# A sorted, alternating list of experts, and TensorE work moved into the waits of the expert stage

## The chip, the cores and the metric

The kernel runs on one core of a Trainium2 chip. The metric is the device time of one execution in microseconds, the median of three runs.

## What is computed

A decoder layer for one sequence of 512 tokens and a width of 1024, all in float32. A first part (modulation from a vector c, a gated recurrence with a causal convolution beside causal pooling, an output projection, the residual sum) leads to `h`, the normed and modulated rows that go into a mixture of experts:

```
logits = h @ router_w + router_b              # 512 x 32
top_val, top_idx = top_k(logits, 4)           # four experts a token
gates = softmax(top_val)
for each expert e, on the rows that chose it:
    u = h_rows @ w1[e] + b1[e]                # 1024 -> 2048
    a = min(u_even, 7) * sigmoid(1.702 * min(u_even, 7)) * (clip(u_odd, -7, 7) + 1)
    y = a @ w2[e] + b2[e]                     # 1024 -> 1024
f = sum over a token's four experts of gate * y
out = x + gate_f * rms_norm(f)
```

512 tokens with 4 choices make 2048 rows, spread unevenly over 32 experts. The number of rows of each expert is known only when the router has run.

## The kernel before, in words

**Ahead of the expert stage.** The first part runs on all engines to about 245 us. Then the routing: VectorE takes the four largest logits of each token, TensorE counts by products with ones and an upper triangle how many rows each expert has and where each row stands in its expert, and VectorE turns this into slots (L1074 to L1095). Rows of one expert are packed into halves of H = 32 rows; two halves are a step of 64. TensorE makes the table of slots (L1393, 16 products that follow the pairs of VectorE operations of L1094 and L1095), VectorE the indices for gathers and scatters (L1124 to L1129, semaphore `idx_ok`). A small table in SBUF, `counts`, has for each expert the steps (row 0), the halves (row 1), the full steps of two halves (row 2), and in row 3 how much the semaphore of its weights rises (16, or 0 for an expert without rows). All engines read it into registers and loop over it.

**The expert stage.** Every engine runs the experts in the order 0 to 31, two to a turn of its loop (`pair` and `slot`), and skips those without rows. For an expert TensorE does, in this order:

- the bias product (L1497): a selection matrix `sel_e`, made by VectorE for this expert (`select`, L1160), times `b1_all`, into bank 7; ScalarE copies it to `b1_cur` (L821);
- for each full step the up products of both halves (`up`, L1418, 32 matmuls a half; each float32 matmul has two records in the profile), and between them the transposes of the next step's gathered rows (`transpose_x`, L1406) and the turn of the first activated half (`turn_first`, L1427);
- for an odd last half its up products, the same transposes, a wait for its activation (`act_ok`) and the turn;
- a register load of the next expert's halves (`load_halves`, L1477);
- for each full step the turn of the second half (`turn(1)`), the down products of the first half (`down`, L1446, 16 matmuls a half, four weight tiles of four), the down products of the second, with the turn for the next step inside; for an odd last half its down products.

VectorE adds the bias, clamps, multiplies and stores the activated half to `act_store` (`activate`, L1139 to L1147), and adds the two parts of each down result (`finish`, L1152 to L1156). ScalarE does the sigmoid, copies turned blocks (`take_gT`, L798) and transposed rows (`take_xT`, L789). GpSimd gathers rows two steps ahead (L575, L580), copies the next two halves into the first two places of `act_store` (L634, semaphore `copied`), and scatters results (L586, L590).

**The weights.** `W1` has two slots of eight tiles of 1 MB; expert e goes into slot e mod 2. SyncE issues them (`load_w1`, L372): tile k waits until the last up half of expert e - 2 has passed tile k (`w1_used`, L359). `W2` has one slot of four tiles of 1 MB; ScalarE issues them (`load_w2`, L377), tile by tile behind the last down half of the expert before (`w2_used`). Expert 0's weights are loaded before the stage. Expert 1 would go to slot 1, which is free: four tiles behind `counts_ok`, four behind `idx_ok`. It has no rows in these inputs, so nothing is loaded for it there.

```
436            sp.wait_ge(counts_ok, 4)
440            load = sp.value_load(counts[0:1, 3, 1:2], min_val=0, max_val=16)
441            with sp.If(load > 0):
443                    load_w1(sp, 1, 1, k)
```

Of the kernel before, what the change touches and what calls it, by code (L numbers as in the profile page):

```python
# [5 lines left out]
def hybrid_layer(nc, x, c, w_ada, b_ada, norm_mix_pre, norm_mix_post, w_in, conv_w, conv_b, gate_a_w, gate_a_b,  # L6
# [10 lines left out]
    P = 128  # L17
    T, D = x.shape[1], x.shape[2]
# [20 lines left out]
    VECS = 72  # L39

# [13 lines left out]
    with ctx:  # L54
# [126 lines left out]
        idx_n = take(NQ).bitcast(i32)  # L181

# [15 lines left out]
        counts = OV[0:1, 6656 - 4 * E:6656].rearrange("p (a e) -> p a e", a=4).bitcast(i32)  # L198
# [92 lines left out]
        b1_in = sem("b1_in")  # L291
        bias_const = sem("bias_const")
# [88 lines left out]
        def _(sp):  # L381
# [43 lines left out]
            load = sp.value_load(counts[0:1, 3, 1:2], min_val=0, max_val=16)  # L425
            with sp.If(load > 0):
                for k in range(HALF):
                    load_w1(sp, 1, 1, k)
            sp.wait_ge(idx_ok, 1)
            with sp.If(load > 0):  # L430
                for k in range(HALF, KT):
                    load_w1(sp, 1, 1, k)
# [6 lines left out]
            sp.reg_add(landed[1], landed[1], load)  # L439
# [14 lines left out]
            with sp.Fori(1, E // 2) as pair:  # L454
                for slot in range(2):
                    e = 2 * pair + slot
                    add_steps(bass.ds(e - 2, 1))
                    load = sp.value_load(counts[0:1, 3, bass.ds(e, 1)], min_val=0, max_val=16)
                    with sp.If(load > 0):
# [5 lines left out]
                        for k in range(KT):  # L465
# [7 lines left out]
                            load_w1(sp, e, slot, k)  # L473
# [18 lines left out]
        def _(pool):  # L492
# [55 lines left out]
            nc.gpsimd.iota(iota_t, [[0, J], [1, H]], base=0, channel_multiplier=0, **IMP).then_inc(route_const, 1)  # L548
            nc.gpsimd.iota(iota_e, [[1, E]], base=0, channel_multiplier=0, **IMP).then_inc(route_const, 1)
# [108 lines left out]
        def _(act):  # L658
# [157 lines left out]
            def expert(e):  # L816
                n_halves = act.value_load(counts[0:1, 1, e], min_val=0, max_val=T // H)
                n_full = act.value_load(counts[0:1, 2, e], min_val=0, max_val=T // (2 * H))
                with act.If(n_halves > 0):
                    act.wait_ge(b1_ps, act.snap(biased, min_val=0, max_val=E) + 1)  # L820
                    nc.scalar.activation(b1_cur, b1_bank[:, :], ACT.Copy).then_inc(b1_ok, 1)  # L821
                    act.reg_add(biased, biased, 1)
# [37 lines left out]
            with act.Fori(0, E - 1) as e:  # L860
                expert(bass.ds(e, 1))
                load = act.value_load(counts[0:1, 3, bass.ds(e + 1, 1)], min_val=0, max_val=16)
                with act.If(load > 0):
# [3 lines left out]
                    for part in range(J):  # L867
# [10 lines left out]
                        load_w2(act, e, part, w2_v[1:E])  # L878
# [18 lines left out]
        def _(dve):  # L897
# [133 lines left out]
            def route_tile(i):  # L1031

                dve.wait_ge(evac, number["logits", i] + 1)
                if i == 0:
                    dve.wait_ge(router_in, 32)
                    dve.wait_ge(route_const, 5)
# [554 lines left out]
```

## Time and profile before

| what | value |
|---|---|
| median of three runs | 1470.37 us (1470.14 to 1477.83) |
| the profiled execution: its own time | 1479.31 us |
| its span, first to last instruction | 1477.6 us |
| TensorE busy | 1231.0 us (83%) |
| VectorE, ScalarE, GpSimd busy | 412.6, 217.1, 276.5 us |
| moved by the DMA queues | 462.84 MB, mean 313 GB/s |
| granted TensorE clock, mean | 0.907 of 2.4 GHz |

Rows of the profile name a source line of the kernel before, the engine, what is written and read, and how often. PE is TensorE, DVE VectorE, ACT ScalarE, POOL GpSimd, SP SyncE. "Idle before" is the time the engine stood still in front of an instruction, with the engine, the tile and the line that ended it. PEclk is the granted clock, 1.00 for 2.4 GHz and 0.50 for 1.2.

### The profile page before, as it was taken

How to read it: one execution, taken by the hardware profiler on the slowest of the kernel's cores; microseconds unless marked ns; L12 is line 12 of the kernel's file. 1: busy time of each engine (PE TensorE's matmuls, PEld its weight loads, DVE VectorE, ACT ScalarE, POOL GpSimd, SP SyncE). 2: the span in 40 equal slices, each digit the busy share in tenths (PEclk: the TensorE clock that was granted, in tenths of full speed). 3: DMA queues.
4: the chain of work that ended last, by engine and by line, in shares of the span. 5: the costliest groups of instructions: out<-in, count | busy, mean ns of one | idle time of the engine just before them, and what ended most of it. 6: DMA issues, size and time to landing. Idle time of an engine off the chain costs nothing.

```text
span 1477.6 us, 28341 instructions
## 1 busy us (share of the span) xinstructions
PE 1231.0 (83%) x8843; PEld 416.9 (28%) x8844; DVE 412.6 (28%) x864; ACT 217.1 (15%) x481; POOL 276.5 (19%) x421
## 2 busy tenths in 40 slices
PE   4999995468998999877757999986799889989961
PEld 1434455112332333221212333321223223322320
DVE  3215336212232232211112222321132222222317
ACT  2108532001110111100001101110011011101101
POOL 3032001201222122211101211321021112211212
PEclk9899995688999999988868999998799999999975
DMA  9882514597659588899999970599998997899354
GB/s 323 308 298 115 235 43 185 222 420 297 243 209 420 226 357 341 361 419 421 419 421 420 419 306 25 236 387 420 400 404 363 421 421 325 328 421 421 139 212 183
DMA packets 77461, 462.84 MB, mean 313 GB/s; under 512 B 11924, under 2 KB 12052, under 8 KB 29312
## 3 DMA queue, kind: packets, MB, share of 16 engines
q1 hardware_dynamic: 49280, 314.72, 52.5%
q10 hardware_dynamic: 17568, 126.14, 20.7%
q0 software_dynamic: 10592, 21.72, 4.3%
q8 instruction: 11, 0.18, 0.1%
q14 instruction: 10, 0.08, 0.0%
HBM read 453.08 MB, written 16.91 MB: 318 GB/s over the span
## 4 chain that ended last, share of the span: by engine, by line
PE 68%; DMA 15%; DVE 6%; SPq 5%; issue 3%; ACT 3%; POOLq 1%; ACTq 0%; POOL 0%; DVEq 0%
PE bank L1418 33%; PE bank L1446 18%; DMA W<-in_expert_w 12%; SPq L372 5%; PE bank L1293 4%; PE bank L1335 4%; PE bank L1427 2%; PE bank L1497 2%; DMA W<-in_w_ada 2%; PE bank L1253 1%; PE bank L1406 1%; DVE W L1217 1%; DVE OV L1139 1%; DMA OV<-h_rows,src_cur 1%; DMA W<-y_rows 1%
## 5 line engine op out<-in xcount | busy, mean ns | idle before, releaser
L1418 PE MATMUL bank<-W,OV 128*32 128x512 f32 x5056 | 577.0, 609 | 50.9 <-DMA W<-in_expert_w 50.9
L1446 PE MATMUL bank<-W,OV 128*32 128x512 f32 x2528 | 320.4, 652 | 46.2 <-ACT OV L798 22.3
L1418 PEld LDWEIGHTS bank<-W,OV 128*32 128x32 f32 x5056 | 157.3, 111 | 444.8 <-issue 362.7
L1139 DVE TENSOR_TENSOR OV<-bank,OV 128x512 f32<-128x512 f32 x79 | 54.6, 692 | 487.1 <-PE bank L1418 481.5
L1446 PEld LDWEIGHTS bank<-W,OV 128*32 128x32 f32 x2528 | 83.4, 117 | 228.1 <-issue 189.7
L1152 DVE COPY OV<-bank 64x512 f32<-64x512 f32 x79 | 54.8, 693 | 298.8 <-PE bank L1446 298.8
L580 POOL DMA_INDIRECT OV<-h_rows,src_cur x104 | 106.3, 1022 | 61.8 <-POOL src_cur L575 42.7
L575 POOL COPY src_cur<-OV 128x2 int32 (+1 forms) x52 | 11.3, 218 | 522.6 <-PE bank L1406 492.9
L793 ACT ACTIVATE OV<-OV 128x256 f32<-128x256 f32 x79 | 35.3, 447 | 466.7 <-DVE OV L1141 456.7
L1427 PE MATMUL bank<-ident,store 128*128 128x128 f32 x216 | 48.8, 314 | 48.8 <-DVE store L1147 47.9
L1293 PE MATMUL bank<-W 128*128 128x512 f32 x192 | 85.1, 596 | 0.0
L798 ACT ACTIVATE OV<-bank 128x256 f32<-128x256 f32 x108 | 40.5, 385 | 204.3 <-PE bank L1427 200.8
L1156 DVE TENSOR_TENSOR OV<-bank,OV 64x512 f32<-64x512 f32 x79 | 53.9, 683 | 20.2 <-DMA y_rows<-OV,dst_cur_a 11.1
L1427 PEld LDWEIGHTS bank<-ident,store 128*128 128x128 f32 x216 | 33.4, 205 | 92.4 <-issue 92.4
L1335 PE MATMUL bank<-W,OV 128*128 128x512 f32 x128 | 56.2, 594 | 0.9 <-issue 0.9
L590 POOL DMA_INDIRECT y_rows<-OV,dst_cur_a x51 | 47.5, 931 | 47.7 <-POOL dst_cur_a L586 41.1
L821 ACT ACTIVATE OV<-bank 128x512 f32<-128x512 f32 x31 | 18.5, 597 | 249.1 <-issue 155.8
L789 ACT ACTIVATE OV<-bank 128x256 f32<-128x256 f32 x102 | 35.8, 373 | 123.9 <-PE bank L1406 123.9
L1293 PEld LDWEIGHTS bank<-W 128*128 128x128 f32 x192 | 35.8, 190 | 48.0 <-issue 47.5
L586 POOL COPY dst_cur_a<-OV 64x1 int32 (+1 forms) x51 | 9.1, 179 | 212.6 <-DVE OV L1156 212.6
L1406 PE MATMUL bank<-ident,OV 128*128 128x128 f32 x204 | 34.4, 292 | 11.8 <-DMA OV<-h_rows,src_cur 11.8
L1497 PE MATMUL bank<-b_all,OV 128*128 128x512 f32 x62 | 38.9, 712 | 5.5 <-DVE OV L1160 5.5
(230 smaller groups left out, 674.2 us busy)
## 6 DMA issues: line engine op xcount, KB each, us to landing
W<-in_expert_w SPq DMA_DIRECT2D x252, 1024.0 KB, 14.8
W<-in_expert_w ACTq DMA_DIRECT2D x120, 1024.0 KB
W<-in_w_ada SPq DMA_DIRECT2D x24, 1024.0 KB, 7.1
W<-y_rows SPq DMA_DIRECT2D x4, 2048.0 KB, 14.7
W<-in_w_in SPq DMA_DIRECT2D x3, 2048.0 KB, 11.6
W<-in_w_out SPq DMA_DIRECT2D x1, 4096.0 KB, 16.1
store<-in_x SPq DMA_DIRECT2D x4, 512.0 KB, 5.2
h_rows<-W POOLq DMA_DIRECT2D x4, 512.0 KB, 3.3
```

The costliest lines, as they stand in the source:

```text
L372: sp.dma_start(W1[:, slot, k, :], w1_v[bass.ds(e, 1), :, k, :].rearrange("e p n -> p (e n)"))\
L580: pool.indirect_dma_start(xg[hf], None, h_rows, bass.IndirectOffsetOnAxis(ap=src_cur[:, hf:hf + 1], axis=0), bounds_check=T * J - 1, oob_i ...
L1139: TTo(u_sb[:, hf, :], bank[hf][:, :], b1_cur, ALU.add).then_inc(u_ok[hf], 1)
L1152: nc.vector.tensor_copy(y_part[hf], bank[4 + hf][YP:2 * YP, :]).then_inc(y_part_ok, 1)
L1156: TTo(y_sb[hf], bank[4 + hf][0:YP, :], y_part[hf], ALU.add).then_inc(y_ok[hf], 1)
L1293: last = mm(ps[:, :], win_ring[:, slot, k, f * P:(f + 1) * P], hT[:, k, :], start=(k == 0), stop=(k == KT - 1))
L1335: last = mm(ps[:, :], catT[:, k, i * P:(i + 1) * P], w_out_sb[:, k, n * 512:(n + 1) * 512], start=(k == FT), stop=(k == FT - 1))
L1406: last = tr(bank[2][:, at:at + P], xg[hf][:, m * P:(m + 1) * P], ident[:, :])
L1418: last = mm(bank[hf][H * j:H * j + H, :], xT[:, hf, k % QM, H * (k // QM):H * (k // QM) + H], W1[:, slot, k, UW * j:UW * j + UW], start=(k ...
L1427: last = tr(gT_bank[hf][:, r * P:(r + 1) * P], act_store[:, hf, r::2], ident[:, :])
L1446: last = mm(bank[4 + hf][H * j:H * j + H, :], gT[:, hf, r, H * c:H * c + H], W2[:, c, r, HW * piece:HW * piece + HW], start=(c == 0), stop ...
L1497: mm(b1_bank[:, :], sel_e[:, slot, :], b1_all[:, :], start=True, stop=True).then_inc(b1_ps, 1)
```

## The change

It has three parts.

**The list.** After the counts of halves, VectorE computes for each expert a place in a list: expert 0 first; of the others with rows the one with r larger ones before it gets place 2r + 2 or, counted from the small end, the next odd place, whichever is less. So odd places hold the smallest, in rising order, and even places the largest, in falling order; experts without rows get no place. Four small matrix products turn this into rows of `counts` by place (row 1 halves, row 3 now the expert's number) and into the first slot of each expert. All engines then run over places; the weights and the bias row are taken by the expert's number. The slot of W1 is the place mod 2.

**The bias product.** It is issued one expert ahead, behind the last up product (and its transposes) of the expert before, once ScalarE has copied the current one.

**The down products.** `turn(1)` comes behind the first two tiles of the first down half, not ahead of them.

Cut to its core:

```diff
@@ SyncE
-            load = sp.value_load(counts[0:1, 3, 1:2], min_val=0, max_val=16)
+            load = steps_of(1)
+            second = expert_at(1)
             with sp.If(load > 0):
                 for k in range(HALF):
-                    load_w1(sp, 1, 1, k)
+                    load_w1(sp, second, 1, k)
...
-                            load_w1(sp, e, slot, k)
+                            load_w1(sp, expert, slot, k)
@@ ScalarE
-                        load_w2(act, e, part, w2_v[1:E])
+                        load_w2(act, following, part)
@@ VectorE, routing
-            link(nc.vector.tensor_copy(exp_f[:, 0, :], exp_i[:, 2, :]))
-            link(nc.vector.tensor_tensor_scan(exp_f[:, 1, :], ones[:, 0:E], exp_f[:, 0, :], 0.0, ALU.mult, ALU.add))
-            link(TTo(exp_f[:, 2, :], exp_f[:, 1, :], exp_f[:, 0, :], ALU.subtract))
-            link(TS(exp_f[:, 3, :], exp_f[:, 2, :], float(2 * H), None, ALU.mult))
+            link(nc.vector.tensor_copy(halves_f, exp_i[0:E, 1, :]))
+            link(STT(key, halves_f, float(E), iota_e[0:E, :], ALU.mult, ALU.subtract))
+            link(nc.vector.memset(key[:, 0:1], -2.0 * E))
...
+            link(TTo(by(7), by(6), by(5), ALU.subtract))
+            link(TS(by(7), by(7), 2.0, -1.0, ALU.mult, ALU.add))
+            link(TS(by(5), by(5), 2.0, 2.0, ALU.mult, ALU.add))
+            link(TTo(by(5), by(5), by(7), ALU.min))
...
+            dve.wait_ge(start_ok, 1)
+            link(TS(exp_f[:, 3, :], bank[6][:, 64:64 + E], float(2 * H), None, ALU.mult))
@@ VectorE, experts
+            def select(i, slot):
+
+                e = dve.value_load(counts[0:1, 3, i], min_val=0, max_val=E - 1)
+                TS(sel_e[:, slot, :], same_j, hot_row[:, bass.ds(e, 1)], None, ALU.mult).then_inc(sel_e_ok, 1)
...
-                    dve.wait_ge(sel_e_ok, dve.snap(e + 1, min_val=1, max_val=E))
+                    dve.wait_ge(b1_ps, dve.snap(e + 1, min_val=1, max_val=E))
                     select(bass.ds(e + 1, 1), 1 - slot)
@@ TensorE
+            def next_bias(e, slot):
+
+                pe.wait_ge(sel_e_ok, pe.snap(e + 2, min_val=2, max_val=E + 1))
+                mm(b1_bank[:, :], sel_e[:, 1 - slot, :], b1_all[:, :], start=True, stop=True).then_inc(b1_ps, 1)
...
-                        pe.wait_ge(sel_e_ok, e + 1)
-                        mm(b1_bank[:, :], sel_e[:, slot, :], b1_all[:, :], start=True, stop=True).then_inc(b1_ps, 1)
+                        pe.reg_add(biased, biased, 1)
...
                             up(0, s, s, slot, range(KT), True, w1_arrived)
                             transpose_x(s + 1)
+                            pe.wait_ge(b1_ok, biased)
+                            next_bias(e, slot)
+                            pe.reg_add(step, step, 1)
+                            load_halves(e + 1)
                             pe.wait_ge(act_ok, before + 1)
                             turn_first()
-                            pe.reg_add(step, step, 1)
-                        load_halves(e + 1)
+                        with pe.If((n_halves & 1) < 1):
+                            load_halves(e + 1)
+                            pe.wait_ge(b1_ok, biased)
+                            next_bias(e, slot)
...
+                                pe.wait_ge(gT_ok[0], now + 1)
+                                down(0, d, range(2), False, w2_arrived)
                                 pe.wait_ge(act_ok, before + 2)
                                 pe.wait_ge(copied, f + 1)
                                 pe.wait_ge(gT_ok[1], f + 1)
                                 turn(1)
-                                pe.wait_ge(gT_ok[0], now + 1)
-                                down(0, d, range(J), False, w2_arrived)
+                                down(0, d, range(2, J), False, w2_arrived)
```

How the instructions stand, at three places. First TensorE, an odd last half of an expert; before (L1418 up, L1406 transposes, L1427 turn, L1477 the register load):

```order
L1418 MATMUL bank<-W,OV 32x512 x32
L1399 ISA
L1406 MATMUL bank<-ident,OV 128x128 x4
L1514 REGISTER_ALU
L1432 ISA
L1427 MATMUL bank<-ident,store 128x128 x2
L1434 ISA
L1510 UNCONDITIONAL_BRANCH
L1477 ISA
L1477 TENSOR_LOAD OV
```

and after (L1481 up, L1469 transposes, L1554 bias, L1540 the register load, L1490 turn):

```order
L1481 MATMUL bank<-W,OV 32x512 x32
L1462 ISA
L1469 MATMUL bank<-ident,OV 128x128 x4
L1553 ISA
L1554 MATMUL bank<-b_all,OV 128x512
L1588 ISA
L1540 TENSOR_LOAD OV
L1540 ISA x3
L1495 ISA
L1490 MATMUL bank<-ident,store 128x128 x2
```

The next expert's bias product and the register load now stand ahead of the turn.

Second TensorE, the down products of a full step; before (L1427 turn, L1446 down):

```order
L1427 MATMUL bank<-ident,store 128x128 x2
L1527 REGISTER_ALU
L1439 REGISTER_ALU
L1446 MATMUL bank<-W,OV 32x512 x16
L1529 REGISTER_ALU
L1446 MATMUL bank<-W,OV 32x512 x8
```

and after (L1509 down, L1490 turn):

```order
L1509 MATMUL bank<-W,OV 32x512 x8
L1603 REGISTER_ALU
L1604 REGISTER_ALU
L1490 MATMUL bank<-ident,store 128x128 x2
L1509 MATMUL bank<-W,OV 32x512 x8
L1608 REGISTER_ALU
L1509 MATMUL bank<-W,OV 32x512 x8
```

The first eight of the sixteen down matmuls of the first half stand ahead of the turn.

Third VectorE, the operations on the counts ahead of the slot numbers; before:

```order
L1077 TENSOR_SCALAR OV<-OV 128x32
L1078 CAST OV<-OV 128x32
L1079 SCALAR_TENSOR_TENSOR OV<-ones,OV 128x32
L1080 TENSOR_TENSOR OV<-OV 128x32
L1081 TENSOR_SCALAR OV<-OV 128x32
L1083 TENSOR_TENSOR OV<-bank,OV 128x96
```

and after, the last of its 23 (the 15 ahead of these are alike, on 32 partitions):

```order
L1123 TENSOR_REDUCE W<-W 32x1
L1125 TENSOR_TENSOR W<-OV,ident 32x32
L1126 TENSOR_REDUCE W<-W 32x1
L1127 SCALAR_TENSOR_TENSOR W<-W,ident 32x1
L1128 COPY W<-W 32x1
L1129 TENSOR_SCALAR W<-OV,W 32x33
L1131 TENSOR_SCALAR W<-bank,W 32x32
L1133 TENSOR_SCALAR OV<-bank 128x32
L1135 TENSOR_TENSOR OV<-bank,OV 128x96
```

Four operations have become 23, and L1131 and L1133 read the results of TensorE products.

## Rows read from the trace of the kernel before

**Rows 1.** The page's costliest groups: TensorE's largest (line, count, busy us, mean ns, idle before)
```profile
L1418 PE MATMUL bank<-W,OV 128*32 128x512 f32 x5056 | 577.0, 609 | 50.9 <-DMA W<-in_expert_w 50.9
```
**Rows 2.** Windows: length, busy us (records) of each engine, PEclk, DMA share, GB/s
```profile
240.00:260.00 20.00, 11.68 (x52) 10.59 (x51) 14.66 (x67) 2.98 (x4) 0.00 (x0) 0.59 0.00 0
...
596.00:877.00 281.00, 219.83 (x1658) 63.96 (x1654) 58.11 (x124) 26.37 (x70) 47.34 (x72) 0.87 1.01 416
...
270.00:1419.00 1149.00, 997.03 (x8066) 305.11 (x8066) 278.93 (x583) 122.26 (x320) 220.77 (x341) 0.92 0.84 345
```
**Rows 3.** Windows of single experts: 3, 6, 8, 11, 17, 18, 21, 26, 29; then 0
```profile
316.27:417.88 101.61, 86.75 (x715) 25.85 (x711) 24.29 (x50) 9.69 (x26) 18.12 (x29) 0.90 0.67 268
...
483.71:542.86 59.15, 57.61 (x513) 18.77 (x509) 17.55 (x36) 7.05 (x19) 13.15 (x21) 1.00 0.67 268
...
579.30:615.74 36.44, 34.90 (x310) 11.50 (x306) 10.57 (x22) 4.37 (x12) 8.47 (x14) 1.00 0.88 360
...
670.46:696.99 26.53, 16.64 (x109) 3.85 (x105) 3.77 (x8) 1.96 (x5) 3.43 (x5) 0.80 1.01 420
...
859.47:964.03 104.56, 103.02 (x916) 33.30 (x912) 31.17 (x64) 12.38 (x33) 23.66 (x38) 1.00 0.42 164
...
964.03:981.64 17.61, 14.41 (x109) 4.34 (x105) 3.70 (x8) 1.96 (x5) 3.95 (x6) 0.90 1.01 418
...
1025.82:1088.85 63.03, 51.83 (x410) 14.66 (x406) 13.30 (x28) 5.86 (x15) 9.00 (x14) 0.86 0.99 408
...
1213.35:1259.95 46.60, 46.60 (x410) 14.71 (x406) 13.99 (x29) 5.92 (x15) 9.76 (x16) 1.00 0.83 342
...
1325.90:1354.83 28.93, 25.24 (x209) 7.56 (x205) 7.14 (x15) 3.23 (x8) 5.07 (x8) 0.94 1.01 421
...
270.87:290.95 20.08, 16.73 (x105) 4.56 (x104) 2.08 (x5) 2.61 (x7) 5.44 (x7) 0.77 0.79 313
```
**Rows 4.** Waits of TensorE: us in total, times, longest
```profile
PE bank L1418 <- DMA W<-in_expert_w: 50.9, 20, 4.2
```
**Rows 5.** Timeline of expert 18 (one half): start, length, engine, line, idle before
```profile
964.03 1.12 PE L1497 MATMUL bank<-b_all,OV 128*128 128x512 f32 x2
...
967.60 0.29 DVE L1160 TENSOR_SCALAR OV<-OV 128x128 f32<-128x128 f32 x1 [1.92 <-issue]
...
974.70 0.50 PE L1427 MATMUL bank<-ident,store 128*128 128x128 f32 x2 [1.95 <-DVE store L1147]
...
975.31 0.38 ACT L798 ACTIVATE OV<-bank 128x256 f32<-128x256 f32 x1 [1.05 <-PE bank L1427]
...
976.45 5.26 PE L1446 MATMUL bank<-W,OV 128*32 128x512 f32 x32 [1.25 <-ACT OV L798]
```
**Rows 6.** Timeline of expert 29 (two halves), TensorE
```profile
1345.55 0.67 PE L1427 MATMUL bank<-ident,store 128*128 128x128 f32 x2 [3.69 <-DVE store L1147]
...
1346.15 6.45 PE L1446 MATMUL bank<-W,OV 128*32 128x512 f32 x48
```
**Rows 7.** Window behind that gap
```profile
1345.50:1348.00 2.50, 2.45 (x14) 0.85 (x18) 0.00 (x0) 0.38 (x1) 0.61 (x1) 0.50 1.03 415
```
**Rows 8.** Timeline of expert 4 (three halves), ScalarE and TensorE
```profile
442.69 0.66 ACT L798 ACTIVATE OV<-bank 128x256 f32<-128x256 f32 x2
...
443.31 5.36 PE L1446 MATMUL bank<-W,OV 128*32 128x512 f32 x48 [1.54 <-ACT OV L798]
```
**Rows 9.** Timeline of VectorE in the routing
```profile
245.96 0.19 DVE L1074 TENSOR_SCALAR OV<-bank 128x32 int32<-128x32 f32 x1 [0.65 <-PE bank L1356]
...
247.54 0.18 DVE L1081 TENSOR_SCALAR OV<-OV 128x32 f32<-128x32 f32 x1
```
**Rows 10.** Chain that ended last, gathers in it: start, length
```profile
267.30 2.62 DMA OV<-h_rows,src_cur
...
838.72 7.45 DMA OV<-h_rows,src_cur
```
**Rows 11.** The page's DMA queues: packets, MB, share
```profile
q0 software_dynamic: 10592, 21.72, 4.3%
```

More of the change, by code:

```diff
@@ L39, in hybrid_layer @@
     VECS = 72
+    NPOS = E + 1
     h_rows = nc.dram_tensor("h_rows", (T * J, QW), fp32).ap()
@@ L181, in hybrid_layer @@
         idx_n = take(NQ).bitcast(i32)
+        take = carver(B_hi[:, KT * T + 3 * D:])
+        by_expert = take(8)
+        steps_by = take(1)
+        key_row, compare, before_row = take(E), take(E), take(E)
+        place = take(NPOS)
+        iota_id = take(1)
         take = carver(OV)
@@ L431, in _ @@
                 for k in range(HALF, KT):
-                    load_w1(sp, 1, 1, k)
+                    load_w1(sp, second, 1, k)
             step, landed = sp.alloc_register("sp_step"), [sp.alloc_register(f"sp_landed{v}") for v in range(2)]
@@ L438, in _ @@
             sp.reg_mov(landed[1], 16)
-            sp.reg_add(landed[1], landed[1], load)
+            with sp.If(load > 0):
+                sp.reg_add(landed[1], landed[1], 16)
+            sp.nop()
             def add_steps(e):
@@ L457, in _ @@
                     add_steps(bass.ds(e - 2, 1))
-                    load = sp.value_load(counts[0:1, 3, bass.ds(e, 1)], min_val=0, max_val=16)
+                    load = steps_of(e)
+                    expert = expert_at(e)
                     with sp.If(load > 0):
@@ L861, in _ @@
                 expert(bass.ds(e, 1))
-                load = act.value_load(counts[0:1, 3, bass.ds(e + 1, 1)], min_val=0, max_val=16)
+                load = act.value_load(counts[0:1, 0, bass.ds(e + 1, 1)], min_val=0, max_val=T // (2 * H))
+                following = act.value_load(counts[0:1, 3, bass.ds(e + 1, 1)], min_val=0, max_val=E - 1)
                 with act.If(load > 0):
@@ L1390, in _ @@
             rank_add(TT - 1, TT - 1).then_inc(rank_ok, 1)
+            pe.wait_ge(place_ok, 1)
+            mm(bank[6][0:E, 0:E], by_expert[0:E, 3:4].to_broadcast([E, E]), ident[0:E, 0:E], start=True, stop=True)\
+                .then_inc(pos_ok, 1)
+            pe.wait_ge(place_ok, 2)
+            pe.wait_ge(rows_ok, 1)
+            mm(bank[6][:, 64:64 + E], steps_by[0:E, :].to_broadcast([E, P]), before_row[0:E, :], start=True, stop=True)\
+                .then_inc(start_ok, 1)
+            for v in range(2):
+                last = mm(bank[5][0:1, 64 + 64 * v:64 + 64 * v + NPOS], by_expert[0:E, v:v + 1], place[0:E, :], start=True,
+                          stop=True)
+            last.then_inc(list_ok, 1)
             for n in range(TK):
@@ L1544, in _ @@
                         load_halves(e + 1)
+                        next_bias(e, slot)
                 pe.nop()
```

65 lines of the change are left out of this document (49 added, 16 removed).

## The prediction

> **What bounds the kernel now.** I read four views, in this order. The grouping by line says where TensorE's time goes [rows 1]: its largest group, the up products (L1418), has 577.0 us of the span, all in the expert stage, which runs from 270 to 1419 us. In that stage TensorE is busy 997 of 1149 us; the DMA queues move 345 GB/s on average, but 416 to 420 GB/s when saturated, and 164 during the largest expert [rows 2, 3]. So neither is the bound alone: long experts leave the queues idle, runs of short ones starve TensorE.
>
> The stretches from one bias product to the next give one expert each [rows 3]. The count of PE records tells its size: 64 up and 32 down records a half of 32 tokens. Counted so, there are 31 experts with tokens and 79 halves: eleven experts of one half, seven of two, seven of three, three of four, one each of five, seven and nine; expert 1 has none. Undisturbed, they take 17.6, 28.9, 36.4, 46.6, 59.2 and 104.6 us. No expert of seven ran undisturbed; a step of two halves costs (104.6 - 59.2)/2 = 22.7, so 81.9. The sum is 11 x 17.6 + 7 x 28.9 + 7 x 36.4 + 3 x 46.6 + 59.2 + 81.9 + 104.6 = **1036 us**. The stage takes 1149, so some **113 us** are stalls: expert 11 stands at 26.5 for 17.6, expert 21 at 63.0 for 46.6, expert 3 at 101.6 for 81.9 [rows 3], and the waits name weights as the first cause [rows 4]. These experts come in or right behind a run of short ones. An expert's weights are 12 MB (12.58 million bytes), 30.0 us at 420 GB/s, whatever its size.
>
> The fourth view is the order of time inside an expert of one half [rows 5] and of two [rows 6]. The first has TensorE idle 1.95 us until VectorE has stored the activation and 1.25 us until ScalarE has copied the turned block; the second 3.69 us in one piece. Behind that gap the granted clock is 0.50, the level of 1.2 GHz [rows 7], and the 48 down records take 6.45 us; an expert of three, whose only gap is 1.54 us, does 48 in 5.36 [rows 8].
>
> **The change, part by part.**
>
> *Routing.* VectorE gets 23 small operations for the list where it had 4, in the chain to the slot numbers. Seven such operations take 1.58 us (245.96 to 247.54), 0.22 each [rows 9]: 19 more are 4.2. One TensorE product, whose result VectorE waits for, adds the 0.65 of such a wait [rows 9]. The six operations for the counts now stand ahead of the 16 slot pairs and seven behind them go: 0. Together **+5 us** before the first gather. Bounds: 2 (small operations on 32 partitions shorter, the product hidden) to 9 (each reduction and product at double). The other new matrix products lie beside VectorE.
>
> *The empty slot.* The list drops expert 1. Before, it left slot 1 of W1 empty, with the queues at 0 GB/s from 240 to 260 [rows 2], and expert 3's weights came only during its up product: 19.7 us of the stalls. Now the second expert's first four tiles load behind the counts, the rest behind the index. I take +2 for the first gather, which has these beside it: 2.62 us in the clear, 7.45 under load [rows 10], so 0 to 5.
>
> *The fills, per expert.* One half: the bias product (one up tile's worth, 1.1 us [rows 5]) goes into the gap of 1.95. The register load of the next count leaves the second gap, where TensorE restarted 0.76 us behind ScalarE's copy (975.31 + 0.38 to 976.45), against 0.29 in an expert of three (442.69 + half of 0.66 to 443.31) [rows 5, 8]: -0.5. If the clock then stays up, the 32 down records take 3.6 (at the rate of the 48 in 5.36) for 5.26; I take half of these 1.7. So 17.6 becomes **15.1** (bounds 14.2 to 17.1). Two halves: bias (1.1) and the first half of the down product (16 records, 1.8) fill 2.9 of 3.69, and the clock has no long gap left, -1.1: 28.9 becomes **25.0** (bounds 24 to 28). Three, five, seven, nine: the gap ends with ScalarE's chain as before, so the bias is saved and the turn that leaves the gap costs about 0.7: -0.4 each. Four: no gap, so 0: the bias product only changes place; +0.5 if the turn's copy is late behind 1.8 us of cover. The new waits stand in TensorE's queue, with the turn, ScalarE's copy and the down product behind them. The early bias product needs VectorE's choice of the next expert's row, made 3.6 us behind the bias product [rows 5], now with one more register load in front; TensorE asks at about 7.7, so it costs 0. TensorE's sum falls to 11 x 15.1 + 7 x 25.0 + 7 x 36.0 + 3 x 46.6 + 58.8 + 81.5 + 104.2 = **977 us**.
>
> *The order.* Expert 0, then smallest and largest in turn; in halves 1, then 1 9 | 1 7 | 1 5 | 1 4 (three times) | 1 3 (four times) | 2 3 (three times) | 2 2 (twice). The queues carry weights and, in the software queues, gathers and scatters: 21.7 MB [rows 11], some 4 of it before the stage, so 0.56 an expert. 12.58 + 0.56 = 13.15 MB are **31.3 us** an expert, 62.6 a pair. On TensorE the pairs take 119, 97, 74, 62, 51, 61 and 50. The buffers reach one expert ahead: a slot of W1 loads once the expert two places before is in its last up half, W2 once the one before is in its last down half. So time saved in the long pairs can't be banked, and from the five on the queues decide:
> - Expert 0 starts at 271 + 5 + 2 = 278 and takes 20.1 (270.87 to 290.95) [rows 3]; its successor 15, and 3 more for its W2, which shares the queues with W1. The expert of nine starts at 316.
> - It, the short ones and the seven: the expert of five starts at 316 + 104 + 15 + 82 + 15 = 532. Its last up half starts 29 later (one step of 22.7, then the first up half of the next 7), at 561, and frees W1 for position 8.
> - From 561 until W1 of the last and W2 of the last but one have landed, the queues carry 23 experts' worth: 23 x 31.3 = 720. I add 10 for moments when both buffers are in use (7 of them behind the five, whose down steps outlast the load). That is 1291.
> - The last expert then still has one up tile, an up half, the turns and the gap, two down halves: 0.9 + 7.0 + 1.5 + 3.7 + 7.7 = 21 us. End **1312**.
>
> The end was 1418.9, so the change saves **107 us**. What follows the stage (58.7 us of the span) stays. The profiled execution goes from 1479.3 (span 1477.6) to 1372; it stands 8.9 above the median of the three runs, so the median goes from 1470.4 to about **1364 us**.
>
> A rule that speaks against this sum: "DMA: Bandwidth & Descriptors" of the Trainium skill (Specifications) puts what one core gets of its memory at about 358 GB/s. The trace stands at 416 over 281 us [rows 2], so I go by the trace; the rule's case is rival 5.
>
> **The rivals.**
> 1. *TensorE stays the bound.* If the queues kept up, the stage would end at 278 + 20 + 977 - 15 = 1260, the time 1311. Against it: 31 experts at 31.3 us are 970, with look-ahead of one. Halfway gives 1335. 5%.
> 2. *Late W2 behind each long expert.* W2 shares the queues with the W1 tiles that the short expert itself frees; expert 11 lost 8.9 us so [rows 3]. For: the saturated pairs. Against: the short expert behind the nine lost nothing. At 8 us for each of the five short experts ahead of the saturated part it is +40: 1404. 12%.
> 3. *The order buys nothing, only the fills do*: each expert waits as before, as the look-ahead is one expert. The empty slot gives 20, the fills some 35 outside the starved runs, routing costs 7: 1470 - 20 - 35 + 7 = 1422. 4%.
> 4. *Slower: each pair stalls as expert 21 did.* Place: the up tiles of the expert behind a short one. Price: 16.4 us [rows 3] in each of 15 pairs, 246 on 1260, so 1506 for the stage and 1557 for the kernel. It outweighs the gain from (1418.9 - 1260)/15 = 10.6 us a pair; my forecast has (1312 - 1260)/15 = 3.5. In its favour: the pairs of 1 and 3 need 51 us on TensorE and 62.6 on the queues, 11 short, but they are four. 2%.
> 5. *A lower ceiling of the memory.* Were it 358 GB/s, the 302 MB behind 561 would take 845 us instead of 720: +125, 1489, slower. Stretches at 416 to 420 [rows 2, 3] speak against it. 1%. This is the rule of the page above.
>
> **How the numbers follow.** The forecast has 76%, the rivals 24%. Faster and slower count from 0.5%, 7 us, about what a measurement of this kernel can tell from no change. The forecast's own bounds: routing and gather 2 to 14 against my 7; idle moments of the queues 0 to 35 against 10; the last expert 17 to 28. That gives 1347 to 1396. To leave out no more than 2 in 10 I take **1342 to 1402**, which holds part of rivals 1 and 2. Faster 0.96, same 0.01, slower 0.03.
>
> **What would show it.** In the changed profile: the first gather some 5 us later; weights moving before it; experts of nine, seven and five without a weight wait; gaps under 1 us before the turn in experts of one and two halves, and their down records at full clock; queues saturated from about 560 to 1290, and TensorE's waits on weights mostly in the pairs of 1 and 3 and among the last four. I'm wrong if the queues show holes of more than 35 us in all behind 561, if a short expert behind a long one waits more than 3 us for W2, or if two-half experts don't fall to 26 us where weights are there.

## The result, and the profile after

The changed kernel takes **1422.24 us** (median of 4 runs, 1418.69 to 1422.49), the kernel before 1470.43 in the same comparison; the ratio is 0.9657 (95% interval 0.9628 to 0.9686). It is faster, as forecast, but saves 48 us where the forecast had about 106, and lies 20 us above the top of the range. The profiled execution took 1422.42 us, with a span of 1420.4.

The page of the kernel after, its span and TensorE's groups of the stage (line, count, busy us, mean ns, idle before):

```profile
span 1420.4 us, 28691 instructions
...
PE 1216.7 (86%) x8855; PEld 421.7 (30%) x8856; DVE 415.9 (29%) x882; ACT 218.3 (15%) x481; POOL 276.5 (19%) x422
...
L1481 PE MATMUL bank<-W,OV 128*32 128x512 f32 x5056 | 571.1, 607 | 4.8 <-issue 4.7
L1509 PE MATMUL bank<-W,OV 128*32 128x512 f32 x2528 | 316.8, 634 | 87.2 <-DMA W<-in_expert_w 69.6 <-ACT OV L822 17.6
...
L1490 PE MATMUL bank<-ident,store 128*128 128x128 f32 x216 | 50.5, 316 | 12.4 <-DVE store L1198 12.4
```

The up products (L1481) answer to [rows 1]. The 50.9 us that they waited for weights [rows 4] are gone. But the down products (L1509) now wait 69.6 us for theirs, W2, and this is the largest wait of the kernel. The list of TensorE's waits after (us in total, times, longest):

```profile
PE bank L1509 <- DMA W<-in_expert_w: 69.6, 24, 4.5
PE bank L1509 <- ACT OV L822: 17.6, 21, 1.0
PE bank L1469 <- DMA OV<-h_rows,src_cur: 14.0, 1, 14.0
PE bank L1490 <- DVE store L1198: 12.4, 11, 1.2
```

The fills did what they were to do: the turn waits 12.4 us for VectorE in all, at most 1.2, where a single expert of two halves had 3.69 [rows 6]. Windows of the kernel after (length, busy us and records of each engine, PEclk, DMA share, GB/s): three stretches and the third up to the end of the loads, the expert of one half at place 9, two stretches for the sum below, the moment at which the last weights but W2 of the last place are in, and three moments in the down products of place 9 and behind them. Places are counted from 0:

```profile
279.00:561.00 282.00, 259.81 (x2144) 82.03 (x2148) 72.98 (x152) 31.72 (x83) 57.82 (x89) 0.95 0.68 274
561.00:818.00 257.00, 234.96 (x1946) 73.37 (x1942) 67.28 (x140) 29.62 (x77) 52.75 (x82) 0.95 0.88 359
818.00:1340.00 522.00, 461.77 (x3798) 145.97 (x3801) 133.37 (x278) 58.79 (x152) 103.42 (x160) 0.95 0.99 409
...
818.00:1328.00 510.00, 450.07 (x3708) 142.50 (x3711) 128.54 (x269) 57.30 (x148) 100.23 (x155) 0.95 1.01 417
...
675.50:698.00 22.50, 15.38 (x104) 4.31 (x105) 3.67 (x8) 1.97 (x5) 3.40 (x5) 0.77 0.97 389
...
579.00:818.00 239.00, 216.96 (x1786) 67.32 (x1782) 63.17 (x130) 27.05 (x70) 49.71 (x78) 0.94 0.90 367
...
579.00:1328.00 749.00, 667.03 (x5490) 209.82 (x5486) 191.72 (x398) 84.36 (x218) 149.94 (x233) 0.95 0.98 401
...
1328.00:1330.00 2.00, 2.00 (x14) 0.40 (x6) 0.88 (x2) 0.00 (x0) 1.45 (x2) 1.00 0.36 144
...
691.20:693.10 1.90, 1.90 (x8) 0.18 (x8) 0.00 (x0) 0.00 (x0) 0.00 (x0) 0.50 1.02 414
696.20:699.80 3.60, 3.58 (x20) 0.79 (x24) 1.38 (x2) 0.00 (x0) 0.00 (x0) 0.50 1.00 419
686.50:689.00 2.50, 2.50 (x16) 0.39 (x15) 0.00 (x0) 0.00 (x0) 0.44 (x1) 0.70 1.01 426
```

The stage runs from 279.0 to 1362.6 us, 1083.6 for 1149 before. Between 561 and 818, where the forecast had the queues saturated, they moved 359 GB/s. Only behind 818 do they reach 409, and 417 if the window ends with the last of these loads at 1328, as much as the 416 of [rows 2].

Where the rest is lost shows inside any expert of one half. The timeline of place 9 after (one half; start, length, engine or queue, line, idle before):

```profile
675.51 7.07 PE L1481 MATMUL bank<-W,OV 128*32 128x512 f32 x64 [0.19 <-issue]
675.76 2.73 ACTq L389 DMA_DIRECT2D W<-in_expert_w  x4
...
676.84 6.48 SPq L384 DMA_DIRECT2D W<-in_expert_w  x8
...
683.01 1.02 PE L1554 MATMUL bank<-b_all,OV 128*128 128x512 f32 x2
...
685.18 0.50 PE L1490 MATMUL bank<-ident,store 128*128 128x128 f32 x2 [1.14 <-DVE store L1198]
...
686.42 2.63 PE L1509 MATMUL bank<-W,OV 128*32 128x512 f32 x16 [0.74 <-ACT OV L822]
...
691.18 1.94 PE L1509 MATMUL bank<-W,OV 128*32 128x512 f32 x8 [2.12 <-DMA W<-in_expert_w]
696.22 1.93 PE L1509 MATMUL bank<-W,OV 128*32 128x512 f32 x8 [3.10 <-DMA W<-in_expert_w]
698.00 1.94 PE L1481 MATMUL bank<-W,OV 128*32 128x512 f32 x8
```

At 675.8 ScalarE issues the four W2 tiles (4 MB) of this very expert; TensorE wants them from 686.4. At 676.8 SyncE issues the eight W1 tiles (8 MB) of place 11, which are wanted two places on, from 746.6. Both go at once through the same queues, and the last W2 tile is there 20.5 us behind the issue of the first (675.76 to 696.22). TensorE loses 2.12 + 3.10 = 5.2 us, and the last sixteen down records and the first ones of the next expert run at 1.2 GHz besides (granted clock 0.50 in 691.20 to 693.10 and from 696.20 on; eight records in 1.93 us). Not all of that is the work of these waits: ahead of them, in 686.50 to 689.00, the granted clock is 0.70 on average already, and the first sixteen down records take 2.63 us. The gap in front of the turn holds the bias product and is down to 1.14 us.

### The profile page after: what moved, and what is told of

It is laid out like the page before. It is cut to its first block, busy times and chain, and to the rows that moved or that the text cites. A ratio compares the mean times of both kernels' runs of the same rounds, so it can differ in the third digit from the quotient of the medians.

```text
span 1420.4 us, 28691 instructions
## 1 busy us (share of the span) xinstructions
PE 1216.7 (86%) x8855; PEld 421.7 (30%) x8856; DVE 415.9 (29%) x882; ACT 218.3 (15%) x481; POOL 276.5 (19%) x422
## 4 chain that ended last, share of the span: by engine, by line
PE 65%; DMA 22%; DVE 5%; ACT 3%; issue 2%; ACTq 1%; POOLq 1%; POOL 0%; DVEq 0%
PE bank L1481 31%; DMA W<-in_expert_w 20%; PE bank L1509 18%; PE bank L1345 4%; PE bank L1387 4%; PE bank L1490 2%; PE bank L1305 2%; DVE W L1269 1%; PE bank L1469 1%; DMA W<-in_w_ada 1%; DMA W<-y_rows 1%; DVE OV L1190 1%; DMA W<-in_pool_scale 1%; PE bank L1436 0%; PE bank L1321 0%
## 5 line engine op out<-in xcount | busy, mean ns | idle before, releaser
L1481 PE MATMUL bank<-W,OV 128*32 128x512 f32 x5056 | 571.1, 607 | 4.8 <-issue 4.7
L1509 PE MATMUL bank<-W,OV 128*32 128x512 f32 x2528 | 316.8, 634 | 87.2 <-DMA W<-in_expert_w 69.6
L1481 PEld LDWEIGHTS bank<-W,OV 128*32 128x32 f32 x5056 | 169.4, 112 | 389.4 <-issue 385.9
L1509 PEld LDWEIGHTS bank<-W,OV 128*32 128x32 f32 x2528 | 74.6, 112 | 258.4 <-issue 154.3
L846 ACT ACTIVATE OV<-bank 128x512 f32<-128x512 f32 x31 | 18.5, 597 | 279.0 <-DMA W<-in_expert_w 155.7
L1490 PE MATMUL bank<-ident,store 128*128 128x128 f32 x216 | 50.5, 316 | 12.4 <-DVE store L1198 12.4
L1490 PEld LDWEIGHTS bank<-ident,store 128*128 128x128 f32 x216 | 34.9, 204 | 75.9 <-issue 75.9
L1469 PE MATMUL bank<-ident,OV 128*128 128x128 f32 x204 | 33.9, 289 | 14.0 <-DMA OV<-h_rows,src_cur 14.0
L1198 DVE TENSOR_TENSOR store<-OV 128x256 f32 x79 | 34.5, 437 | 13.9 <-DVE OV L1195 13.9
```

The lines of the kernel that those rows point to most:

```text
L1469: last = tr(bank[2][:, at:at + P], xg[hf][:, m * P:(m + 1) * P], ident[:, :])
L1481: last = mm(bank[hf][H * j:H * j + H, :], xT[:, hf, k % QM, H * (k // QM):H * (k // QM) + H], W1[:, slot, k, UW * j:UW * j + UW], start=(k ...
L1490: last = tr(gT_bank[hf][:, r * P:(r + 1) * P], act_store[:, hf, r::2], ident[:, :])
L1509: last = mm(bank[4 + hf][H * j:H * j + H, :], gT[:, hf, r, H * c:H * c + H], W2[:, c, r, HW * piece:HW * piece + HW], start=(c == 0), stop ...
```

## The experiments

In the first eight the kernel before took 1481.8 and 1482.4 us, in the last four 1469.3; ratios are to these. The two groups ran on different chips, and kernels of different groups can't be compared to better than 12 us. A comparison by ratio assumes that a kernel differs between the groups as the kernel before does. But the changed kernel took 1422.2 us beside a kernel before of 1470.4, and 1420.9 beside one of 1482.4. So where groups are compared both the ratio and the time are given, and what only one of them shows stays open.

**Is it the order of W2 and W1 in the queues?** SyncE holds the W1 tiles of place e back until W2 of the expert now at work (place e - 2) has landed:

```diff
                         sp.reg_add(landed[slot], landed[slot], 16)
+                        sp.wait_ge(w2_in[J - 1], sp.snap(16 * (e - 1), min_val=16, max_val=16 * E))
+                        apart(sp)
```

> The changed kernel, with SyncE holding back the W1 tiles for the place two ahead until W2 of the current place has landed. Theory A (the short experts wait because their W2 shares the queues with W1 tiles that nobody needs for another 50 us): the waits on W2 at places 3 to 13 (28 us, with the clock lost behind them about 40) nearly go, and since W1 never waits in the changed kernel there is nothing to lose: 1375 to 1400 us against 1422. Theory B (W2 is late by its own length: it is issued at the end of the long expert and 4 MB need 10 us): the waits stay as they are, 1418 to 1426. Theory C (from place 13 on the queues' total decides, so what is won ahead of it comes back there as waits on W1): 1405 to 1417.

Measured: **1399.24 us** (1398.04 to 1404.02), ratio 0.9452 (0.9429 to 0.9475); the changed kernel, run again beside the second four, took 1420.94 (below). So some 22 us come back from one wait on a queue. The timeline of place 9 with the hold:

```profile
655.38 3.37 ACTq L389 DMA_DIRECT2D W<-in_expert_w  x4
...
666.04 2.78 PE L1510 MATMUL bank<-W,OV 128*32 128x512 f32 x24 [0.74 <-issue]
...
669.53 1.07 PE L1510 MATMUL bank<-W,OV 128*32 128x512 f32 x8 [0.71 <-DMA W<-in_expert_w]
...
669.95 4.74 SPq L384 DMA_DIRECT2D W<-in_expert_w  x6
```

W2 is complete 14.2 us behind the issue of its first tile instead of 20.5, TensorE waits 0.71 us instead of 5.2, and eight down records take 1.07 us, not 1.93. This expert lasts 16.2 us (22.5 in the changed kernel); those at places 3 and 5 last 14.3 (19.1 and 18.7). Place 13 starts at 781.5 us; the changed kernel has it at 817.9, and the forecast's own terms up to there give 776 (532 + 58.8 + 3 x 15.1 + 3 x 46.6). But of these 36 us only 22 to 23 are left at the last expert's start (1315.9 for 1338.5): the hold has lost 14 us again. Windows (from place 13 on up to the last of the loads that the sum counts) and waits with the hold:

```profile
561.00:781.50 220.50, 211.81 (x1794) 69.83 (x1788) 63.08 (x130) 27.06 (x70) 50.45 (x78) 0.98 0.97 395
781.50:1305.50 524.00, 457.50 (x3740) 143.49 (x3740) 130.49 (x274) 58.82 (x151) 102.25 (x157) 0.94 0.99 406
```

```profile
PE bank L1510 <- DMA W<-in_expert_w: 51.9, 21, 4.6
```

The queues are busy from 561 on (share 0.97 to 0.99), and of the 51.9 us of W2 waits left 48 lie behind place 14, 22 of them in the pairs of one and three, where the weights of a pair take longer than its work, the rest at the experts of two halves. But from 781.5 on they move 406 GB/s, where the changed kernel moved 417 behind 818. Over 524 us that is 14 us: what is lost again is what the queues fall short beside the hold. The time lies at the upper end of theory A's range, and theory C's mechanism has a part in it, though with waits on W2 and none on W1.

**What the list and the fills are worth alone.** The list stays, the fills are undone (the bias product at the border, the turn ahead of the first down product):

```diff
                             transpose_x(s + 1)
-                            pe.wait_ge(b1_ok, biased)
-                            next_bias(e, slot)
-                            pe.reg_add(step, step, 1)
-                            load_halves(e + 1)
                             pe.wait_ge(act_ok, before + 1)
                             turn_first()
...
-                                down(0, d, range(2), False, w2_arrived)
                                 pe.wait_ge(act_ok, before + 2)
...
                                 turn(1)
-                                down(0, d, range(2, J), False, w2_arrived)
+                                down(0, d, range(J), False, w2_arrived)
...
                         pe.reg_add(halves_before, halves_before, n_halves)
+                        pe.wait_ge(b1_ok, biased)
+                        next_bias(e, slot)
```

> The list of the changed kernel with TensorE's order of before: the bias product at an expert's border, the turn ahead of the first down half. If the fills are worth on TensorE what the prediction said (some 60 us over all experts) and nothing hides it: 1480. If most of it only makes the short experts wait longer for W2: 1428 to 1440.

Measured: 1431.74 us (1428.20 to 1438.22), ratio 0.967 (0.9637 to 0.9703). The waits of TensorE without the fills:

```profile
PE bank L1490 <- DVE store L1198: 46.9, 18, 3.8
PE bank L1509 <- DMA W<-in_expert_w: 32.0, 11, 4.2
```

With the fills the first is 12.4 and the second 69.6: 34.5 us of gaps closed, 37.6 us of waits on W2 opened. The fills are worth 59 us on TensorE by the forecast's sums (1036 - 977) and 11 in the kernel's time. The expert behind the nine (place 3) shows it alone: without the fills it waits nothing for W2, with them 3.6 us.

Next the fills and the new routing, but the places numbered as the experts are, the empty one with its place:

```diff
-            link(STT(by(3), ident[0:E, 0:1], 0.0, by(5), ALU.is_equal, ALU.mult))
+            link(nc.vector.tensor_copy(by(3), iota_id[0:E, :]))
```

> The fills and the new routing, but every expert at the place of its own number, the empty one included, as before. The prediction's third rival gives 1470 - 35 + 5 = 1440. If the fills are nearly all lost to weights: 1460 to 1475.

Measured: 1471.06 us (1469.36 to 1473.72), ratio 0.9927 (0.9911 to 0.9944). The fills are nearly all lost to weights. TensorE's waits on weights here (first fence), and in the kernel before for the down products (second fence; the up products have 50.9 us, [rows 4]):

```profile
PE bank L1481 <- DMA W<-in_expert_w: 63.3, 24, 4.2
PE bank L1509 <- DMA W<-in_expert_w: 38.7, 15, 4.2
```

```profile
PE bank L1446 <- DMA W<-in_expert_w: 19.2, 8, 4.3
```

That is 102 us for 70. And experts by number, with only the empty one dropped:

```diff
-            link(STT(key, halves_f, float(E), iota_e[0:E, :], ALU.mult, ALU.subtract))
+            link(TS(key, halves_f, 1.0, float(E), ALU.min, ALU.mult))
+            link(TTo(key, key, iota_e[0:E, :], ALU.subtract))
...
-            link(TS(by(7), by(7), 2.0, -1.0, ALU.mult, ALU.add))
+            link(TS(by(7), by(7), 64.0, -1.0, ALU.mult, ALU.add))
...
-            link(TS(by(5), by(5), 2.0, 2.0, ALU.mult, ALU.add))
+            link(TS(by(5), by(5), 1.0, 1.0, ALU.mult, ALU.add))
```

> The changed kernel with the experts in order of number, the empty one dropped, no sorting (the key is the same for all with rows). Against the run with all experts at their own numbers it shows the empty slot alone, against the changed kernel the sorting alone. Prediction's terms: 20 us for the empty slot, so 1420, and the sorting some 55 more on top. If sorting costs W2 waits at each short expert as fast as it removes W1 waits: within 10 us of the changed kernel's 1422.

Measured: 1455.16 us (1453.75 to 1457.24), ratio 0.982 (0.9804 to 0.9837). The ladder in these first four is then 1481.8, with the fills and the routing 1471.1 (-10.7), with the empty place dropped 1455.2 (-15.9). The rest, some 34 us, is the sorting. Neither expectation came true: the empty place is worth 16 us for 20, the sorting 34 for 55. The sorting is read against the unaltered changed kernel, which ran beside the next four:

> The changed kernel unaltered, for a ratio to the kernel before on this chip, since runs on another chip gave the kernel before 1482 us and not 1470. All theories: a ratio of 0.963 to 0.969.

Measured: 1420.94 us (1418.30 to 1421.87), ratio 0.9576 (0.956 to 0.9592); the kernel before took 1482.4 there. So the ratio missed the expected 0.963 to 0.969. The changed kernel repeats within 1.3 us, while the kernel before differs by 12 between the groups.

**Where TensorE's own time stands.** All weight loads of the stage's loops are left out (those ahead of the loops stay):

```diff
-                            load_w1(sp, expert, slot, k)
+                            sp.sem_inc(w1_in[slot][k], 16)
...
-                        load_w2(act, following, part)
+                        act.sem_inc(w2_in[part], 16)
```

> The changed kernel without the weight loads of the expert stage's loops (W1 from place 2 on, W2 from place 1 on; the semaphores are raised as if they had landed, and the products use what lies in SBUF). It leaves TensorE's own time. The prediction's sum of 977 us, and a stage of some 280 to 1260, gives a ratio to the kernel before of 0.90 (about 1322 us where before has 1470). If the fills do not save what the sum says (1036 stays): 0.94.

Measured: 1317.01 us (1315.80 to 1321.91), ratio 0.8892 (0.8872 to 0.8912). Its stage in one window:

```profile
281.00:1256.00 975.00, 938.07 (x8062) 313.75 (x8060) 278.62 (x582) 122.60 (x318) 217.94 (x337) 0.99 0.08 20
```

The forecast had 977 for TensorE's sum. By kinds: one half 14.3 to 16.0 us (forecast 15.1), two 25.3 mostly (25.0), three 35.9 (36.0), four 47.0 (46.6), five 58.6 (58.8), seven 81.3 (81.5), nine 104.0 (104.2). These terms hold. Now only W2's loads are left out, W1's stay:

```diff
-                        load_w2(act, following, part)
+                        act.sem_inc(w2_in[part], 16)
```

> The changed kernel without the loads of W2 from place 1 on (its semaphore is raised, the down products use expert 0's tiles); all W1 loads stay. Theory A and B say that W1 never is late and only W2 is waited for: the same time as without any load, ratio 0.90 to 0.91, as W1 alone needs 20 us an expert. If the queues' total were what counts, W1 would be waited for in the pairs of 1 and 3: 0.92 or more.

Measured: 1324.86 us (1320.83 to 1326.39), ratio 0.8927 (0.8907 to 0.8947): 8 us above the kernel with no loads, and its list of waits has none of TensorE on expert weights. W1's 8 MB are never late by themselves.

**Holding more.** Besides the first hold, W1's tiles 4 to 7 wait until W2 of place e - 1 has landed too:

```diff
                         for k in range(KT):
+                            if k == 4:
+                                sp.wait_ge(w2_in[J - 1], sp.snap(16 * e, min_val=32, max_val=16 * E))
+                                apart(sp)
```

> As the run that holds W1 of the place two ahead behind W2 of the current place (ratio 0.945), and its tiles 4 to 7 also behind W2 of the next place. That run still waited 5 to 8 us for W2 from place 15 on. If that is W2 sharing the queues with the rest of W1: these waits fall to about 2 us and the ratio to 0.93. If the queues' total is the bound there, the waits move to W1 and the ratio stays at 0.945; if the hold leaves the queues idle while both buffers wait, it rises to 0.955.

Measured: 1492.07 us (1481.14 to 1499.38, 10 runs), ratio 1.006 (1.0038 to 1.0082), 0.6% slower than before. None of the three expectations had that. Its waits of TensorE:

```profile
PE bank L1485 <- DMA W<-in_expert_w: 104.1, 37, 4.3
...
PE bank L1513 <- DMA W<-in_expert_w: 13.3, 5, 4.0
```

The down products (L1513) hardly wait, but the up products (L1485) wait 104.1 us. For a long expert, place e - 1 is a short one whose W2 isn't even issued until the long one before it is in its last down half. The second half of W1 then has only the 14 to 16 us of the short expert to come in, behind 4 MB of W2.

The last four ask where the hold should end, and what it rests on. One waits for W2's third tile instead of the fourth (`w2_in[2]`):

```diff
-                        sp.wait_ge(w2_in[J - 1], sp.snap(16 * (e - 1), min_val=16, max_val=16 * E))
+                        sp.wait_ge(w2_in[2], sp.snap(16 * (e - 1), min_val=16, max_val=16 * E))
```

> As the run that holds W1 of the place two ahead behind W2 of the current place (1399 us), but only until the third of W2's four tiles has landed. If the queues run dry for a moment at each such hold (they stood at 399 GB/s behind 800 us instead of 413): 1385 to 1395. If the fourth tile then comes as late as without the hold: 1400 to 1420.

Measured: **1388.37 us** (1386.77 to 1390.06), ratio 0.945 (0.9437 to 0.9463). And one for the second (`w2_in[1]`, otherwise the same line):

> The same until the second tile has landed. Between the run with the third tile and the changed kernel's 1421: if holes in the queues cost more than the lateness of two tiles, 1380 to 1395; if the lateness counts, 1400 to 1420.

Measured: 1391.20 us (1389.73 to 1393.50), ratio 0.9468 (0.9455 to 0.9481). Windows and waits with the third tile:

```profile
561.00:775.00 214.00, 205.67 (x1755) 68.08 (x1757) 61.52 (x127) 27.32 (x71) 47.87 (x75) 0.99 0.96 395
780.70:1293.00 512.30, 454.09 (x3736) 144.59 (x3740) 130.49 (x274) 58.59 (x151) 102.28 (x157) 0.95 1.01 417
```

```profile
PE bank L1510 <- DMA W<-in_expert_w: 46.1, 18, 4.5
```

The third tile's ratio equals the fourth's (0.945 and 0.9452), though the runs stand 11 us apart, as the kernel before does between the groups. The traces speak for the third: place 13 starts at 780.7 us (781.5 with the fourth), the last expert at 1303.8 (1315.9), and in between the queues move 417 GB/s for 406, so they no longer fall short. This is what the expectation of 1385 to 1395 rested on. But the unaltered changed kernel has no run in this group, so how much of the 11 us is the tile's stays open. The third is better than the second by 2.8 us; the runs overlap (up to 1390.06 and from 1389.73), so I don't rest anything on it. **The version with the hold on the third tile beats both kernels.**

Does the hold help without the sorting? Experts by number, the empty one dropped, with the hold on the fourth tile (the edits of the fourth and the first experiment together):

> Experts in order of number without the empty one, with W1 held behind W2 of the current place. Unsorted and without the hold it was 1455. If the hold helps wherever a short expert waits for W2: 1435 to 1445 (40 us of W2 waits there, of which those in the runs of short experts come back as waits on W1). If the hold only makes sense in a sorted list, since in a run of short experts W1 itself is late: 1455 to 1475.

Measured: 1455.48 us (1454.19 to 1459.04), ratio 0.9903 (0.9888 to 0.9918): the same time as without the hold (1455.16), and worse by the ratio (0.982). Either way the hold gives nothing here. TensorE's waits without the hold (first fence) and with it (second):

```profile
PE bank L1482 <- DMA W<-in_expert_w: 47.9, 17, 4.2
PE bank L1510 <- DMA W<-in_expert_w: 40.5, 14, 4.5
```

```profile
PE bank L1483 <- DMA W<-in_expert_w: 64.5, 23, 4.2
PE bank L1511 <- DMA W<-in_expert_w: 32.7, 14, 4.7
```

Down waits (second lines) fall by 8, up waits (first lines) grow by 17: in a run of short experts W1 is soon wanted too. In these runs the hold paid in the list where a long expert follows each short one, and not in the order of numbers. And the fills undone, with the hold on the fourth tile (the edits of the second and the first):

> The sorted list with the hold and TensorE's order of before. Without the hold the fills made 1431 into 1421. If the fills were hidden there behind waits on W2 at the short experts, they are worth more with the hold: 1420 to 1430 against 1399. If the queues' total hides them: 1405 to 1412.

Measured: 1408.67 us (1402.88 to 1413.42), ratio 0.9595 (0.9579 to 0.9611). The kernel with this hold and the fills is of the other group: by the medians (1399.24) the fills are worth 9 us here, by the ratios (0.9452) 1.4%, some 20; without the hold they were worth 11 by the medians. The range of these runs is wide, 10 us. So whether the late W2 hid a part of the fills in the total stays open. Ahead of place 13 the traces show that it did. Its first up products without the fills, with the hold (first fence) and without it (second):

```profile
792.33 7.07 PE L1482 MATMUL bank<-W,OV 128*32 128x512 f32 x64
```

```profile
813.02 7.07 PE L1481 MATMUL bank<-W,OV 128*32 128x512 f32 x64
```

With the fills they start at 781.5 (780.7 on the third tile, in this group) and at 817.9 us: with the hold the fills gain 11 us up to there, without it they lose 5.

## Why the prediction was wrong

**What held.** The routing and the first gather: the last operation on the index started at 269.44 us for 264.10 before, +5.3 for a forecast of 5. The gather beside the new W1 loads took 6.31 us for 2.62, in the chain that ended last after:

```profile
272.65 6.31 DMA OV<-h_rows,src_cur
```

That is +3.7 where I took +2 (bounds 0 to 5), and TensorE starts at 279.0, 9.0 later, for 7. The empty slot was 19.7 us before and its removal bought 15.9. TensorE's sum of 977 is 975 in the run without loads; the terms by kind are within 0.9 us. Rival 1's time, 1311, was 1317.0 there. The waits on W1 went, as forecast. Four experts of the pairs of one and three (places 14 to 20) start 62.6, 61.9 and 61.6 us apart, for the forecast's 62.6 a pair by bytes: behind 818 the queues are the bound.

**What failed** is the step that the queues' total decides from the expert of five on, with "10 for moments when both buffers are in use" for all their idleness. The end came at 1362.6 for 1312, and the 51 us lie in three steps:
- Ahead of the five, +18. It starts at 549.9 for 532: 2 from the start, 2 from expert 0, 2 from the nine and the seven. The other 12 are the short experts at places 1, 3 and 5: 22.2, 19.1 and 18.7 us, where the sum had 18, 15 and 15, with waits on W2 of 3.4, 3.6 and 3.3. The sum had 3 for such a wait at place 1 and nothing at places 3 and 5.
- The queues from then on, +19. The five's last up half starts at 549.9 + 29 = 579. From there the sum has 720 + 10 = 730 until the weights that it counts are in; they were in at about 1328, 749 later, at 401 GB/s. 749 us at 401 are 300 MB (forecast 302), 715 us at the 420 of [rows 3]: the queues stood still, or ran below that, for 34 us, not 10. Nearly all of it lies ahead of 818: there 239 us at 367 GB/s would be 209 at 420, 30 less.
- The tail, +14. Behind 1328 I had 21 us, the last expert alone. TensorE was still in the last but one, which had begun at 1314.1 and took its 24.4; the last began at 1338.5 and took 24.1. So the weights that came last were W2 of the last but one, and not W1 of the last.

The median missed by 58 us, not 51. The other 8 are a subtraction: the profiled execution of the kernel before stood 8.9 us above its median, and the forecast took the same off again. That of the changed kernel took 1422.42 us, 0.2 above its median. And the forecast's own bounds, added, give 1345 to 1403, not 1347 to 1396; the measured 1422 lies above either.

The first two have one mechanism, and the hold shows it for the larger part: W2 of a short expert, wanted within 11 us, shares the queues with W1 of the place after next, wanted a long expert later. With W1 held back place 13 starts at 781.5 us, against 776 by the forecast's terms and 817.9 without it. The stage then ends at 1340.2 for 1362.6, and at 1327.9 with the hold on the third tile, in the other group: 22 and 35 us of the 51. The price is paid twice: TensorE waits, and it also frees the buffers later, so that the queues stand idle in the long expert behind. The hold lifts 561 to 818's 359 GB/s to 395 in the same part of the work.

**The rival that came true is the second**, late W2 at short experts, and it had 12%. Its place was right, its form too narrow: I priced 8 us at each of five short experts ahead of the saturated part (1404), and took it that there a wait costs nothing, as the queues decide anyway. It happened at every short expert from place 1 to 19: 3.2 to 3.6 us up to the one behind the five, 5.2 to 6.6 behind the fours, 7.7 to 8.0 behind the threes. What I held against it, an expert behind the nine that lost nothing [rows 3], was the wrong witness. Before the change it wanted its W2 later, by the gaps that the fills then closed: in the sorted list without the fills the expert behind the nine doesn't wait either, and with them it waits 3.6 us, though the queues are all but idle ahead of it (35 GB/s from 410 to 427 us). I had the right one too, expert 11 at 26.5 us, in the same rows. That the kernel crossed a line I had set (a short expert behind a long one waiting over 3 us for W2; holes over 35 us behind 561, where 257 us at 359 GB/s are 37 more than at 420) says the same.

**The third rival** came nearest in time (1422), for a wrong reason: the order is worth some 34 us, the fills 11 and the empty place 16, for 0, 35 and 20, and they come off the 1482 us that the kernel before took there.

What stays open: with the hold on the fourth tile the last expert still starts 28 us later than the forecast has it (1315.9; 1312 less the 24 of the last expert), on the third 16. Up to place 13 it is 5 in both; the rest lies behind it, where the queues move 406 and 417 GB/s. The tail's 14 us have no experiment of their own. No run separates the moments when both buffers are in use from gathers and scatters in between.

## What to carry to other kernels

Count not only how many bytes the queues must move but whose turn it is: two queues that issue at once share the rate, so a transfer that is wanted next took nearly half as long again beside one that is wanted much later. When you shorten the work in front of a wait, ask first what will be late next; here the fills closed 34.5 us of gaps and opened 37.6 us of waits on W2. A hold on the transfer that isn't urgent is one wait on one queue and was worth 22 us by the medians (1.3% by the ratios), but only where the held one has slack: held twice it cost 71 us against the changed kernel, and in an order that had used up the slack it gave nothing.

## What the runs showed of the hardware

- 4 MB of W2 took 20.5 us from the first issue to the use of the last tile beside the 8 MB of W1 that another queue issued 1.1 us later, and 14.2 us when that was held. The later, larger transfer doesn't stand behind the earlier one.
- The kernel before took 1470.4, 1481.8, 1482.4 and 1469.3 us in four comparisons, the changed one 1422.2 and 1420.9 in two of them. The second and third were on one chip, the fourth on another. How much a change gains can so depend on where it is measured: here 3.4% and 4.2%.
- "DMA: Bandwidth & Descriptors" of the Trainium skill (Specifications) puts what one core gets from its memory at about 358 GB/s, the rate of a memory stack halved between its two cores. The trace after has 417 GB/s over 510 us, so for this kernel, which runs on one core, the measurement decides; no run here has both cores at work. Rival 5 was not what happened, though the 359 GB/s between 561 and 818 look like it. The hold moves 395 in that part of the work, so that was no ceiling.
